# A two-layer fp32 trunk on one core: the decay's narrow projection taken from the normed tiles, within the third value group

## The chip, the core and the metric

One core of one Trainium2 chip. The metric is the device time of one execution in microseconds, as a median over runs. All values are fp32, and the result has to have fp32 accuracy, which decides how products are formed (below).

## The reference, cut to what matters

A trunk of two layers. Each layer has a feed-forward part, a mixer stage with four branches (convolution, retention, gated linear attention, differential attention over a paged cache), and another feed-forward part. It works on 592 tokens: 64 of samples, 16 meta tokens, 512 of a prompt. The mixer stage starts with one projection of the normed activations, of which the gated branch's decay takes 16 columns:

```python
x = rmsnorm(h, w['norm_mix'])
z = x @ w['w_in'] + w['b_in']
(c_a, c_g, r_q, r_k, r_v, r_g, g_q, g_k, g_v, g_r, g_low,
 d_q, d_k, d_v, gates) = jnp.split(z, split_at, axis=-1)
...
g_pre = (g_low @ w['gla_alpha_w'] + w['gla_alpha_b']).astype(jnp.float32)
gla_decay = (jax.nn.log_sigmoid(g_pre) / GLA_TAU).reshape(B, L, GLA_HEADS, GLA_DK)
```

`g_low` has 16 columns; it is the narrow projection that is meant here.

## The kernel before

**Layout.** Activations lie transposed: 128 partitions by 8 blocks (KD) of 592 tokens (T). A product of fp32 accuracy is made from parts: a tile x is split into `x_hi` (rounded) and `x_lo` (the rest), weights likewise into `w_hi` and `w_lo`, and TensorE makes hi x hi, hi x lo and lo x hi in a fast format. The narrow projection is the exception: its weights `low_raw` are whole fp32, and TensorE multiplies them in its whole-fp32 form. Its 592 tokens are cut into four strips of 148, and strip r takes the 32 columns of the array, and the 32 output rows, from 32 r on. PSUM has eight banks; a pair of them holds a product of 592 tokens.

**Queues.** Every engine runs a list written out by hand, with waits on semaphores between them. A wait stops everything behind it on its engine. Weights come in units of 128 x 1024 through a ring of four slots: SyncE loads, ScalarE makes `w_hi` (`split_high`, L814), VectorE makes `w_lo` (`split_low`, L2063).

**The stage around the change** is `project(l)`, which every engine has; it runs once for each layer, at 423 to 500 us and again some 1391 us later.

- TensorE: three value groups of 256 columns each, over five windows of tokens. Products of a group go to banks (5 g + w) mod 8 (L1626). Group 0 works with activations that aren't scaled by the norm. Group 1 as well. Group 2 runs block by block: for each block k, 15 matmuls (five windows by three parts), and then it signals `x_taken`, since nobody needs the unscaled block k any more. Then come tiles 0 to 3 of the transposed projections (`tile(l, c)`, L1420), each 48 matmuls into a bank pair, tile c into pair min(c, 3). Then the narrow projection (L1677) into bank 0: for each of 8 blocks, for x_hi and x_lo, four strips; 64 matmuls. Then tile 4 (`Z_FIRST`), which takes pair 3 like tile 3 and waits for ScalarE's eviction of tile 3. Then sums of squares for the attention's norms (L1432).
- VectorE: evicts the five windows of each group with scale and bias (L2425), then splits two weight units. Behind group 1's splits it runs `renorm(l)`: for each block it writes the normed tile, whole, into one of three rooms `fresh[k % 3]` (L2087), and once ScalarE has copied it rounded to `x_hi` (L855, behind `x_taken`), it makes `x_lo` for block k-1 (L2081). Then group 2's evictions.
- ScalarE: `renorm` copies; `split_high` of two units; eviction of tiles 0 to 3 (L1082), each followed by a `split_high`; then a wait for the narrow product, its eviction in four strips to `GL` (L1100), and then the squares of tiles 0 to 3 (L1117), which open the attention.
- GpSimd loads the value bias and `low_raw` at the start of the stage (L714, L715).

TensorE's narrow block and its neighbours:

```python
                pe.wait_ge(low_loaded, 16)
                pe.wait_ge(z_ready, 1)
                for k in range(KD):
                    for n, xp in enumerate((x_hi, x_lo)):
                        for r in range(4):
                            mm = pe.matmul(ps[32 * r:32 * r + 32, 0, 0:STRIP], low_raw[:, k, :], xp[:, k, STRIP * r:STRIP * r + STRIP].bitcast(F32),
                                           start=k == 0 and n == 0, stop=k == KD - 1 and n == 1)
                mm.then_inc(low_product, 1)
```

Of the kernel before, what the change touches and what calls it, by code (L numbers as in the profile page):

```python
# [19 lines left out]
F32 = mybir.dt.float32  # L20
# [4 lines left out]
ACT = mybir.ActivationFunctionType  # L25
# [5 lines left out]
KD, KF = D // P, FF // P  # L31
# [3 lines left out]
T = TS + META + SEQ  # L35
# [89 lines left out]
Z_FIRST, Z_BEFORE = 4, 6  # L125
# [73 lines left out]
def build(nc, h_in, wstream, wlow, params, vbias, cache_k, cache_v, page_table, st_ret, st_gla,  # L199
# [9 lines left out]
    with ExitStack() as ctx:  # L209
        def sem(name):  # L210
            return ctx.enter_context(nc.semaphore(name))
# [7 lines left out]
        def keep(name, shape, dt=F32):  # L219
            nonlocal at  # L220
            t = place(name, shape, dt, at)
            at += -(-4 * int(np.prod(shape[1:])) // 32) * 32
            return t

        hT = keep("hT", [P, KD, T])
        x_hi = keep("x_hi", [P, KD, T], F32R)
        x_lo = keep("x_lo", [P, KD, T], F32R)
# [94 lines left out]
        GL = V[96:112, 0, 0:T]  # L322
        inverse_room, fresh = Z[:, 10, :], (Z[:, 11, :], Z[:, 12, :], Z[:, 13, :])
# [8 lines left out]
        kpage = area("kpage", [P, 2, PAGES, 2 * P], 0)  # L332
        vpage = area("vpage", [P, 2, PAGES, 256], 16384)
        low_raw = area("low_raw", [P, 8, 32], 32768)
        STRIP = T // 4
        vb = area("vb", [P, 768], 45056)
        s_bias = area("s_bias", [P, PAST + NT], 32768)
        new_bias = area("new_bias", [P, 4, TS], 36896)
# [78 lines left out]
        ps = ctx.enter_context(nc.psum_tensor("ps", [P, 8, 512], F32))  # L417
# [19 lines left out]
        normed = sem("normed")  # L437
# [25 lines left out]
        def msem(name):  # L463
            cleared.append(sem(name))
            return cleared[-1]

        v_products, v_ready, z_ready = msem("v_products"), msem("v_ready"), msem("z_ready")
        low_loaded, low_product = msem("low_loaded"), msem("low_product")
# [338 lines left out]
        def _(act):  # L807
# [280 lines left out]
            def project(l):  # L1088
                act.wait_ge(mixers_open, l + 1)
                act.sem_inc(phases_entered, 1)  # L1090
                norm(l, 1)
                for c in range(-6, -2):
                    tile(l, c)
                renorm(l)
                for c in range(-2, Z_FIRST):
                    tile(l, c)
                act.wait_ge(low_product, 1)
                for r in range(4):
                    r0 = 32 * r
                    ins = act.activation(GL[:, STRIP * r:STRIP * r + STRIP], ps[r0:r0 + 16, 0, 0:STRIP], ACT.Identity,  # L1100
                                         bias=prm[r0:r0 + 16, P_ZB + NZ:P_ZB + NZ + 1])
                ins.then_inc(z_ready, 1)

            def exps(x):
                n = META if x < H else P
# [303 lines left out]
        def _(pe):  # L1409
# [170 lines left out]
            def tile(l, c):  # L1580

                pos = c + 6
                unit_ready(l * QUADS + U_MIX // RING + pos // RING, pos % RING)
                if c == Z_FIRST:
                    pe.wait_ge(z_ready, Z_FIRST)
                elif c == Z_FIRST + 1:
                    pe.wait_ge(z_ready, Z_FIRST + 1)
                    pe.wait_ge(root_logs, 3)
                elif c == Z_BEFORE:
                    pe.wait_ge(z_ready, Z_FIRST + 2)  # L1590
                elif c > Z_BEFORE:
                    pe.wait_ge(z_ready, c + 1)
                if c:
                    products(z_pair(c), pos % RING, (0, 8), 0, x_hi, x_lo).then_inc(units_multiplied, 1)
                else:
                    for k in range(KD):
                        pe.wait_ge(x_ready, l * 16 + 8 + k + 1)
                        last = products(0, pos % RING, (k, k + 1), k, x_hi, x_lo, start=k == 0, stop=k == KD - 1)
                    last.then_inc(units_multiplied, 1)
# [17 lines left out]
            def project(l):  # L1617
                pe.wait_ge(mixers_open, l + 1)
                pe.sem_inc(phases_entered, 1)

                def values(g, w, k):

                    c0, n = window(w)
                    s0 = 2 * g % RING
                    for m, (xp, wp) in enumerate(((x_hi, w_hi), (x_hi, w_lo), (x_lo, w_hi))):
                        mm = pe.matmul(ps[0:n, (WINDOWS * g + w) % 8, 0:256], xp[:, k, c0:c0 + n], wp[:, s0:s0 + 2, k, :],  # L1626
                                       start=k == 0 and m == 0, stop=k == KD - 1 and m == 2)
                    return mm

                def value_done(mm, w):  # L1630
                    mm.then_inc(*((v_products, 1) if w < WINDOWS - 1 else (units_multiplied, 2)))

                unit_ready(l * QUADS + U_MIX // RING, 1)
                pe.wait_ge(x_ready, l * 16 + KD - 1)
                for k in range(KD):
                    if k == 3:
                        pe.wait_ge(squares_summed, 8 * (l * 3 + 2))
                        sum_tile(3, ones[:, 0, :], ssum)
                        for w in range(WINDOWS):
                            c0, n = window(w)  # L1640
                            mm = pe.matmul(ps[0:n, 5, w:w + 1], ssum[:, c0:c0 + n], ones[:, 0, 0:1], start=True, stop=True)
                        mm.then_inc(square_total, 1)
                    if k == KD - 1:
                        pe.wait_ge(x_ready, l * 16 + KD)
                    for w in range(WINDOWS):
                        mm = values(0, w, k)
                        if k == KD - 1:
                            value_done(mm, w)
                pe.wait_ge(norm_steps, 2 * (l * 3 + 1) + 1)
                pe.wait_ge(token_steps, 2)  # L1650
                unit_ready(l * QUADS + U_MIX // RING, 3)
                for w in range(WINDOWS):
                    if WINDOWS + w >= 8:
                        pe.wait_ge(v_ready, WINDOWS + w - 7)
                    for k in range(KD):
                        mm = values(1, w, k)
                    value_done(mm, w)
                unit_ready(l * QUADS + U_MIX // RING + 1, 1)
                pe.wait_ge(v_ready, 3 * WINDOWS - 8)
                for k in range(KD):  # L1660
                    for w in range(WINDOWS):
                        mm = values(2, w, k)
                        if k == KD - 1:
                            value_done(mm, w)
                    if k < KD - 1:
                        mm.then_inc(x_taken, 1)
                pe.wait_ge(v_ready, 2 * WINDOWS)
                tile(l, 0)
                pe.wait_ge(v_ready, 3 * WINDOWS)
                for c in range(1, Z_FIRST):  # L1670
                    tile(l, c)
                pe.wait_ge(low_loaded, 16)
                pe.wait_ge(z_ready, 1)
                for k in range(KD):
                    for n, xp in enumerate((x_hi, x_lo)):
                        for r in range(4):
                            mm = pe.matmul(ps[32 * r:32 * r + 32, 0, 0:STRIP], low_raw[:, k, :], xp[:, k, STRIP * r:STRIP * r + STRIP].bitcast(F32),  # L1677
                                           start=k == 0 and n == 0, stop=k == KD - 1 and n == 1)
                mm.then_inc(low_product, 1)

            prompt_heads = [(j, h) for j in range(WINDOWS) for h in range(H)]

# [349 lines left out]
            for n, c in enumerate(range(0, RL, 512)):  # L2032
                mm = pe.matmul(ps[0:16, 4 + n, 0:min(512, RL - c)], rb[0:33, :], bucket[0:33, c:min(c + 512, RL)], start=True, stop=True)
            mm.then_inc(bias_row_made, 1)
            for n in range(SQUARED_FIRST):
                pe.wait_ge(squared, n + 1)
                mm = sum_tile(1, ident[:, :], square_rooms[:, n, :], start=n == 0, stop=n == SQUARED_FIRST - 1)
# [19 lines left out]
        def _(v):  # L2057
# [16 lines left out]
            def renorm(l):  # L2074

                v.wait_ge(norm_steps, 2 * (l * 3 + 1) + 2)

                def low(k):
                    v.wait_ge(x_high, 16 * l + 8 + k + 1)
                    v.wait_ge(normed, 8 * l + k + 1)  # L2080
                    v.tensor_tensor(x_lo[:, k, :], fresh[k % 3], x_hi[:, k, :].bitcast(F32), ALU.subtract).then_inc(x_ready, 1)  # L2081

                for k in range(KD):
                    c = P_GAIN + 8 + k
                    if k >= 3:
                        v.wait_ge(x_ready, 16 * l + 8 + k - 2)
                    v.scalar_tensor_tensor(fresh[k % 3], hT[:, k, :], prm[:, c:c + 1], inverse_room, ALU.mult, ALU.mult).then_inc(normed, 1)  # L2087
                    if k:
                        low(k - 1)
                low(KD - 1)  # L2090
# [341 lines left out]
            def tile(l, c):  # L2432

                pos = c + 6
                split_low(l * QUADS + U_MIX // RING + pos // RING + 1, pos % RING)
# [741 lines left out]
```

## Time and profile before

| | |
|---|---|
| median of 3 runs | 2790.12 us |
| lowest, highest | 2789.74, 2792.55 us |
| the profiled execution, first to last instruction | 2789.1 us |
| TensorE busy | 2767.2 us (99%) |
| VectorE busy | 1986.8 us (71%) |
| ScalarE busy | 1206.8 us (43%) |
| mean granted clock of TensorE | 0.998 |
| one layer's narrow block on the chain | 4.16 us |

The rows further down come from one profiled execution, in microseconds from its first instruction. PE is TensorE's matmul, PEld its weight load, DVE VectorE, ACT ScalarE, POOL GpSimd. L1677 is line 1677 of the kernel. In a timeline a row gives the start, the length, and how many instructions are merged into it; matmuls overlap in the array, so a matmul's length is more than its distance to the next. A matmul of whole fp32 leaves two records. An entry in brackets is the engine's idle time before the row and who ended it. The chain is the work that ended last, followed back from the end of the kernel.

### The profile page before, as it was taken

What the parts mean: (1) busy time and instruction counts of PE and PEld (TensorE: products, weight loads), DVE (VectorE), ACT (ScalarE), POOL (GpSimd) and SP (SyncE); (2) the same over time, 40 slices, a digit from 0 to 9 for tenths busy, and PEclk for the clock granted to TensorE, in tenths of its full rate; (3) what the DMA queues carried; (4) which work ended last, traced back from release to release, by engine and by line L of the source; (5) the groups of instructions that cost most, each with busy time, mean ns of one, the idle gap of its engine ahead of it and who ended that gap; (6) DMA issues with size and microseconds to landing.
All of it is one profiled execution on the core that took longest, in us unless ns stands there. A gap on an engine that the chain in (4) does not pass through costs nothing.

```text
span 2789.1 us, 57776 instructions
## 1 busy us (share of the span) xinstructions
PE 2767.2 (99%) x21828; PEld 2687.1 (96%) x21828; DVE 1986.8 (71%) x3589; ACT 1206.8 (43%) x2160; POOL 128.2 (5%) x234
## 2 busy tenths in 40 slices
PE   8999999999999999999999999999999999999999
PEld 7999999998899999999999999999888999999999
DVE  8889534478667688887488895344787676899952
ACT  6445323435435254445254453234354343544521
POOL 0000001230000000000000000012300000000000
PEclk9999999999999999999999999999999999999999
DMA  4222326463234312223212223255733343122233
GB/s 138 91 95 98 108 75 198 155 202 131 98 117 172 140 64 91 90 90 114 91 67 92 90 98 106 68 198 163 214 118 121 108 178 130 61 92 103 98 106 103
DMA packets 104815, 325.92 MB, mean 117 GB/s; under 512 B 15055, under 2 KB 31855, under 8 KB 103104
## 3 DMA queue, kind: packets, MB, share of 16 engines
q1 hardware_dynamic: 91728, 280.67, 29.2%
q0 software_dynamic: 12912, 42.86, 4.8%
q8 instruction: 118, 1.93, 0.3%
q14 instruction: 57, 0.47, 0.1%
HBM read 291.45 MB, written 30.94 MB: 116 GB/s over the span
## 4 chain that ended last, share of the span: by engine, by line
PE 98%; DVE 1%; ACT 1%; issue 0%; DMA 0%; DVEq 0%; ACTq 0%; POOLq 0%
PE ps L1420 52%; PE ps L1449 35%; PE ps L1626 3%; PE ps L1432 1%; PE ps L1695 1%; PE ps L1911 1%; PE ps L1747 1%; PE ps L1728 1%; PE ps L1775 0%; PE ps L1795 0%; PE ps L1677 0%; PE ps L1737 0%; PE ps L1851 0%; PE ps L1934 0%; PE ps L1777 0%
## 5 line engine op out<-in xcount | busy, mean ns | idle before, releaser
L2063 DVE TENSOR_TENSOR w_lo<-w_raw,w_hi 128x1024 fp32r<-128x1024 f32 x240 | 292.7, 1224 | 353.0 <-ACT w_hi L814 349.4
L1449 PE MATMUL ps<-x_more,w_hi 128*128 128x296 f32 (+1 forms) x2112 | 456.8, 298 | 1.2 <-DVE x_more L2927 0.8
L1449 PE MATMUL ps<-x_hi,w_hi 128*128 128x296 f32 (+1 forms) x1408 | 420.0, 298 | 1.2 <-DVE w_lo L2101 1.2
L1449 PE MATMUL ps<-x_hi,w_lo 128*128 128x296 f32 (+1 forms) x1408 | 420.4, 299 | 0.0
L1449 PE MATMUL ps<-x_lo,w_hi 128*128 128x296 f32 (+1 forms) x1408 | 420.4, 299 | 0.0
L814 ACT ACTIVATE w_hi<-w_raw 128x1024 fp32r<-128x1024 f32 x224 | 234.9, 1053 | 407.2 <-PE ps L1420 240.1
L1420 PE MATMUL ps<-x_hi,w_hi 128*128 128x296 f32 (+1 forms) x1600 | 362.4, 308 | 3.8 <-ACT hT L1162 3.8
L2101 DVE TENSOR_TENSOR w_lo<-w_raw,w_hi 128x512 fp32r<-128x512 f32 x440 | 296.6, 690 | 88.4 <-ACT w_hi L862 85.8
L1449 PEld LDWEIGHTS ps<-x_more,w_hi 128*128 128x128 f32 x2112 | 351.0, 188 | 2.4 <-issue 1.3
L1420 PE MATMUL ps<-x_hi,w_lo 128*128 128x296 f32 (+1 forms) x1600 | 347.3, 299 | 0.0
L1420 PE MATMUL ps<-x_lo,w_hi 128*128 128x296 f32 (+1 forms) x1600 | 347.2, 298 | 0.0
L1449 PE MATMUL ps<-x_more,w_lo 128*128 128x296 f32 (+1 forms) x1056 | 314.6, 298 | 0.0
L1420 PE MATMUL ps<-hid_hi,w_hi 128*128 128x296 f32 (+1 forms) x1408 | 309.4, 299 | 0.0
L1420 PE MATMUL ps<-hid_lo,w_hi 128*128 128x296 f32 (+1 forms) x1408 | 307.8, 297 | 0.0
L1420 PE MATMUL ps<-hid_hi,w_lo 128*128 128x296 f32 (+1 forms) x1408 | 307.8, 297 | 0.0
L912 ACT ACTIVATE p_copy<-ps 128x296 f32<-128x296 f32 (+1 forms) x264 | 109.7, 416 | 389.2 <-PE ps L1449 388.8
L1420 PEld LDWEIGHTS ps<-x_hi,w_hi 128*128 128x128 f32 x1600 | 257.7, 189 | 20.1 <-issue 15.8
L862 ACT ACTIVATE w_hi<-w_raw 128x512 fp32r<-128x512 f32 x440 | 265.4, 623 | 14.1 <-PE ps L1420 13.4
L1449 PEld LDWEIGHTS ps<-x_hi,w_hi 128*128 128x128 f32 x1408 | 265.8, 189 | 2.0 <-DVE w_lo L2101 1.7
L1449 PEld LDWEIGHTS ps<-x_hi,w_lo 128*128 128x128 f32 x1408 | 265.9, 189 | 0.1
L1449 PEld LDWEIGHTS ps<-x_lo,w_hi 128*128 128x128 f32 x1408 | 265.1, 188 | 0.0
L1420 PEld LDWEIGHTS ps<-x_hi,w_lo 128*128 128x128 f32 x1600 | 260.2, 189 | 0.0
(378 smaller groups left out, 4926.9 us busy)
## 6 DMA issues: line engine op xcount, KB each, us to landing
w_raw<-wstream SPq DMA_DIRECT2D x420, 512.0 KB, 3.6
kpage<-cache_k SPq DMA_DIRECT2D x128, 128.0 KB, 3.1
vpage<-cache_v POOLq DMA_DIRECT2D x128, 128.0 KB, 3.8
gate_rows<-hT SPq DMA_DIRECT2D x48, 296.0 KB, 2.3
d_sg<-gate_rows SPq DMA_DIRECT2D x16, 888.0 KB, 5.3
h_rows<-hT SPq DMA_DIRECT2D x2, 2368.0 KB, 9.5
hT<-h_rows SPq DMA_DIRECT2D x2, 2368.0 KB, 8.7
hT<-h_in SPq DMA_DIRECT2D x4, 592.0 KB, 8.3
```

The lines of the kernel that those rows point to most:

```text
L814: act.activation(w_hi[:, slot, :, :], w_raw[:, slot, :, :], ACT.Copy).then_inc(weights_high, 1)
L862: act.activation(w_half(t)[0], w_source(t, g, total), ACT.Copy).then_inc(operands_high, 1)
L912: act.activation(room[:, 0:span()], ps[:, bank, 0:span()], ACT.Copy).then_inc(pair_taken, 1)
L1420: mm = pe.matmul(ps[:, 2 * p + half, 0:cols], wp[:, k, :], xp[:, k0 + k - blocks[0], half * cols:(half + 1) * cols], start=start and k == ...
L1432: mm = pe.matmul(ps[:, 2 * p + half, 0:span()], mat, tile[:, half * span():(half + 1) * span()], start=start, stop=stop)
L1449: mm = pe.matmul(ps[:, bank, 0:span()], wp[:, k, :], xp, start=new and k == 0 and n == 0, stop=k == KH - 1 and n == 2, skip_group_check=True)
L1626: mm = pe.matmul(ps[0:n, (WINDOWS * g + w) % 8, 0:256], xp[:, k, c0:c0 + n], wp[:, s0:s0 + 2, k, :], start=k == 0 and m == 0, stop=k == KD ...
L1695: mm = pe.matmul(ps[0:n, score_bank(j, g, i), 0:min(ns, 512)], q, k[:, 0:min(ns, 512)], start=True, stop=True)
L1728: mm = pe.matmul(ps[r0:r0 + 32, part, :], q, kpage[:, b2, 4 * part:4 * part + 4, P * j:P * j + P], start=True, stop=True)
L1747: pe.matmul(ps[r0:r0 + 32, 5, 0:P], s_turn[:, s, r0:r0 + 32], vpage[:, b2, s, P * j:P * j + P], start=s == 0, stop=False)
L2063: v.tensor_tensor(w_lo[:, slot, :, :], w_raw[:, slot, :, :], w_hi[:, slot, :, :].bitcast(F32), ALU.subtract).then_inc(weights_low, 1)
L2101: v.tensor_tensor(lo, w_source(t, g, total), hi.bitcast(F32), ALU.subtract).then_inc(weight_steps, 1)
```

## The change

The block of 64 narrow matmuls behind tile 3 is gone. Instead, within the third value group, TensorE issues behind the 15 value matmuls of block k four narrow matmuls of block k, which read the normed tile whole from VectorE's room `fresh[k % 3]` and accumulate in bank 7; there are 32 in a layer. Before each portion TensorE waits for the room of its block (`normed`), before the first also for the loaded weights and for the eviction of bank 7. Each portion signals `low_product`, and VectorE waits for it before it writes over a room. ScalarE evicts the narrow product ahead of tile 0 instead of behind tile 3, so the counts that `z_ready` is waited for shift by one, and tile 3, which takes bank 7, waits for that eviction. Everything else stays as it was.

```diff
@@ -332,7 +332,7 @@
         kpage = area("kpage", [P, 2, PAGES, 2 * P], 0)
         vpage = area("vpage", [P, 2, PAGES, 256], 16384)
         low_raw = area("low_raw", [P, 8, 32], 32768)
-        STRIP = T // 4
+        STRIP, LOW_BANK = T // 4, 7
         vb = area("vb", [P, 768], 45056)
         s_bias = area("s_bias", [P, PAST + NT], 32768)
         new_bias = area("new_bias", [P, 4, TS], 36896)
@@ -1092,14 +1092,16 @@
                 for c in range(-6, -2):
                     tile(l, c)
                 renorm(l)
-                for c in range(-2, Z_FIRST):
+                for c in range(-2, 0):
                     tile(l, c)
-                act.wait_ge(low_product, 1)
+                act.wait_ge(low_product, KD)
                 for r in range(4):
                     r0 = 32 * r
-                    ins = act.activation(GL[:, STRIP * r:STRIP * r + STRIP], ps[r0:r0 + 16, 0, 0:STRIP], ACT.Identity,
+                    ins = act.activation(GL[:, STRIP * r:STRIP * r + STRIP], ps[r0:r0 + 16, LOW_BANK, 0:STRIP], ACT.Identity,
                                          bias=prm[r0:r0 + 16, P_ZB + NZ:P_ZB + NZ + 1])
                 ins.then_inc(z_ready, 1)
+                for c in range(Z_FIRST):
+                    tile(l, c)
 
             def exps(x):
                 n = META if x < H else P
@@ -1581,8 +1583,10 @@
 
                 pos = c + 6
                 unit_ready(l * QUADS + U_MIX // RING + pos // RING, pos % RING)
-                if c == Z_FIRST:
-                    pe.wait_ge(z_ready, Z_FIRST)
+                if c == Z_FIRST - 1:
+                    pe.wait_ge(z_ready, 1)
+                elif c == Z_FIRST:
+                    pe.wait_ge(z_ready, Z_FIRST + 1)
                 elif c == Z_FIRST + 1:
                     pe.wait_ge(z_ready, Z_FIRST + 1)
                     pe.wait_ge(root_logs, 3)
@@ -1664,19 +1668,19 @@
                             value_done(mm, w)
                     if k < KD - 1:
                         mm.then_inc(x_taken, 1)
+                    if k == 0:
+                        pe.wait_ge(low_loaded, 16)
+                        pe.wait_ge(v_ready, LOW_BANK + 1)
+                    pe.wait_ge(normed, 8 * l + k + 1)
+                    for r in range(4):
+                        mm = pe.matmul(ps[32 * r:32 * r + 32, LOW_BANK, 0:STRIP], low_raw[:, k, :], fresh[k % 3][:, STRIP * r:STRIP * r + STRIP],
+                                       start=k == 0, stop=k == KD - 1)
+                    mm.then_inc(low_product, 1)
                 pe.wait_ge(v_ready, 2 * WINDOWS)
                 tile(l, 0)
                 pe.wait_ge(v_ready, 3 * WINDOWS)
                 for c in range(1, Z_FIRST):
                     tile(l, c)
-                pe.wait_ge(low_loaded, 16)
-                pe.wait_ge(z_ready, 1)
-                for k in range(KD):
-                    for n, xp in enumerate((x_hi, x_lo)):
-                        for r in range(4):
-                            mm = pe.matmul(ps[32 * r:32 * r + 32, 0, 0:STRIP], low_raw[:, k, :], xp[:, k, STRIP * r:STRIP * r + STRIP].bitcast(F32),
-                                           start=k == 0 and n == 0, stop=k == KD - 1 and n == 1)
-                mm.then_inc(low_product, 1)
 
             prompt_heads = [(j, h) for j in range(WINDOWS) for h in range(H)]
 
@@ -2084,6 +2088,7 @@
                     c = P_GAIN + 8 + k
                     if k >= 3:
                         v.wait_ge(x_ready, 16 * l + 8 + k - 2)
+                        v.wait_ge(low_product, k - 2)
                     v.scalar_tensor_tensor(fresh[k % 3], hT[:, k, :], prm[:, c:c + 1], inverse_room, ALU.mult, ALU.mult).then_inc(normed, 1)
                     if k:
                         low(k - 1)
```

## Rows read from the trace of the kernel before

**Rows 1.** The page's first lines and the chain by engine: busy time (share), share of the chain.

```profile
span 2789.1 us, 57776 instructions
...
PE 2767.2 (99%) x21828; PEld 2687.1 (96%) x21828; DVE 1986.8 (71%) x3589; ACT 1206.8 (43%) x2160; POOL 128.2 (5%) x234
...
PE 98%; DVE 1%; ACT 1%; issue 0%; DMA 0%; DVEq 0%; ACTq 0%; POOLq 0%
```

**Rows 2.** Waits of TensorE, 425 to 700 us: total, times, longest.

```profile
PE ps L1420 <- ACT hT L1162: 1.9, 3, 0.9
```

**Rows 3.** The chain in order of time, 425 to 600 us: start, us, what.

```profile
467.97 26.25 PE ps L1420 x192
494.21 4.16 PE ps L1677 x128
498.38 6.76 PE ps L1420 x48
```

**Rows 4.** Timeline of TensorE around the narrow block: start, us, line, operation, count.

```profile
493.78 0.43 PE L1420 MATMUL ps<-x_lo,w_hi 128*128 128x296 f32 x2
494.14 0.46 PE L1677 MATMUL ps<-x_hi,low_raw 128*32 128x148 f32 x8
...
497.94 0.43 PE L1677 MATMUL ps<-x_lo,low_raw 128*32 128x148 f32 x8
498.31 0.54 PE L1420 MATMUL ps<-x_hi,w_hi 128*128 128x296 f32 x2
498.69 0.43 PE L1420 MATMUL ps<-x_hi,w_lo 128*128 128x296 f32 x2
```

**Rows 5.** Timeline of TensorE, third value group: first matmuls of blocks 0 and 1.

```profile
453.73 0.28 PE L1626 MATMUL ps<-w_hi,x_hi 128*80 128x256 f32 x1
...
455.46 0.28 PE L1626 MATMUL ps<-w_hi,x_hi 128*80 128x256 f32 x1
```

**Rows 6.** Timeline of VectorE as the third value group begins.

```profile
455.09 2.36 DVE L2063 TENSOR_TENSOR w_lo<-w_raw,w_hi 128x1024 fp32r<-128x1024 f32 x2 [0.67 <-ACT w_hi L814]
457.37 1.58 DVE L2087 SCALAR_TENSOR_TENSOR Z<-hT,prm,Z 128x592 f32<-128x592 f32 x2
459.02 0.78 DVE L2081 TENSOR_TENSOR x_lo<-Z,x_hi 128x592 fp32r<-128x592 f32 x1
459.71 0.83 DVE L2087 SCALAR_TENSOR_TENSOR Z<-hT,prm,Z 128x592 f32<-128x592 f32 x1
```

**Rows 7.** Timeline of ScalarE: copies of the rooms, eviction of tile 3.

```profile
458.29 1.45 ACT L855 ACTIVATE x_hi<-Z 128x592 fp32r<-128x592 f32 x2 [2.29 <-DVE Z L2087]
...
494.25 0.76 ACT L1082 ACTIVATE Z<-ps,prm 128x592 f32<-128x592 f32 x1 [4.86 <-PE ps L1420]
```

**Rows 8.** Timelines of VectorE and ScalarE at the same two places, second layer.

```profile
1848.33 1.58 DVE L2087 SCALAR_TENSOR_TENSOR Z<-hT,prm,Z 128x592 f32<-128x592 f32 x2
...
1885.21 0.76 ACT L1082 ACTIVATE Z<-ps,prm 128x592 f32<-128x592 f32 x1 [4.86 <-PE ps L1420]
```

**Rows 9.** Timeline of TensorE: value products behind the one-column products.

```profile
430.75 0.33 PE L1626 MATMUL ps<-w_hi,x_hi 128*80 128x256 f32 x1
430.91 0.28 PE L1626 MATMUL ps<-w_lo,x_hi 128*80 128x256 f32 x1
```

**Rows 10.** Stretches: length, busy PE PEld DVE ACT POOL, granted clock, DMA share, GB/s.

```profile
737.00:740.00 3.00, 3.00 (x13) 2.78 (x13) 1.98 (x5) 0.14 (x1) 0.00 (x0) 0.50 0.02 5
740.00:744.00 4.00, 4.00 (x26) 3.15 (x25) 0.81 (x2) 0.00 (x0) 0.00 (x0) 0.54 0.64 197
2126.00:2129.50 3.50, 3.50 (x17) 3.22 (x18) 2.10 (x5) 0.00 (x0) 0.00 (x0) 0.51 0.08 13
```

**Rows 11.** The chain, 722 to 748 us.

```profile
737.83 3.26 PE ps L1420 x12
```

**Rows 12.** GpSimd's issue of the narrow weights, and its us to landing.

```profile
429.50 0.54 POOL L715 DMA_DIRECT2D low_raw<-wlow  x1
...
low_raw<-wlow POOLq DMA_DIRECT2D x1, 128.0 KB, 10.7
```

## The prediction, made before the changed kernel ran

> **What bounds the kernel now.** I read the page first. TensorE is busy 99% of a span of 2789.1 us and holds 98% of the chain that ended last [rows 1]. In such a kernel a microsecond counts only if TensorE loses or gains it. The waits of TensorE say whether later slack could swallow a loss. From 425 to 700 us, which is the first layer's projection and attention, their longest account is 1.9 us for ScalarE's L1162, in three pieces, and what else it waited for is shorter than a microsecond [rows 2]. Nothing behind the projection waits for a DMA, so a delay of TensorE there moves the end by the same amount.
>
> Then I read the chain through the projection, in order of time [rows 3]. Tiles 0 to 3 take 26.25 us, 6.56 each, the narrow projection 4.16 us (128 records; every whole fp32 matmul leaves two, so 64 matmuls), and tile 4 behind it 6.76 us, 0.20 more than a tile that follows a tile. The second layer does the same 1390.96 us later, to 0.01 us [rows 6 to 8]. So I work out one layer and double it. The profiled span is 1.0 us under the median of 2790.12, so differences carry over as they are.
>
> **Removed: the block behind tile 3.** 64 matmuls go, with both of their transitions: 4.16 + 0.20 = 4.36 us a layer.
>
> **Added: 32 matmuls in eight portions.** The old block shows the price of a portion. Sixteen rows of four matmuls (eight records) start between 494.14 and 497.94, 15 steps of 0.253 us [rows 4]. Eight portions cost 8 x 0.253 = 2.03 us. Using the normed tile whole therefore saves 2.0 us of streaming; moving it has to be paid from that.
>
> **Added: eight ways into the 32-column form and out of it, where there was one.** The old block shows one such passage. The last pair of tile 3 starts at 493.78; pairs are 0.274 apart (6.56 / 24), so the next would start at 494.05, but the first narrow matmul starts at 494.14: 0.09. On the way out, the last portion starts at 497.94 and would be through at 498.19; tile 4 starts at 498.31: 0.12. Its first pair takes 0.38 to the next instead of 0.27: 0.11 [rows 4]. The first portion is also 0.03 longer. Together 0.35 us. The floor is the other change of form in this stage, from one-column products back to the value products: their first start-to-start is 0.16 instead of 0.12, some 0.05 [rows 9], though these keep 80 or more columns of the array. Between 0.05 and 0.35 I take 0.30, near the narrow block's own passage, a little less because a value product streams 256 columns against weights of 80 behind each portion. Eight passages: 2.4 us (0.4 to 2.8).
>
> The Trainium skill, TensorEngine Tiling, section Tiling Modes, has a rule against this change: going from one tiling mode to another drains the array. A full drain at both ends is a rival below. Page and rows agree that each passage costs something; the page names no price.
>
> **Added: the wait for the first normed tile.** In the third value group TensorE now waits, behind block 0 of the values, for the first of VectorE's rooms. Block 0 starts at 453.73 and block 1 at 455.46 [rows 5], so the first portion would start at about 455.55. VectorE's order is unchanged: it first splits two weight units from 455.09 (2.36 us), and the first room is started at 457.37 and, at 0.83 for a room, done by 458.20; ScalarE, which waits for that same room, starts on it at 458.29 [rows 6, 7]. TensorE can be released no earlier: 458.29 - 455.55 = 2.75 us a layer. Queued behind that wait are all other blocks of values and tile 0. I see no work that covers it; before, TensorE ran through block 0 and block 1 without needing the rooms at all.
>
> From block 1 on nobody should wait. A TensorE block becomes 1.73 + 0.25 + 0.30 = 2.3 us. VectorE needs for a step one room (0.75 from start to start) and one low part (0.78), and between them lies ScalarE's copy of 0.70, so from the freeing of x_hi[k-2] to room k it is 0.09 + 0.70 + 0.78 + 0.83 = 2.4 us, while TensorE takes 4.6 for the same two blocks [rows 6, 7]. VectorE's added wait (room k mod 3 is not overwritten before portion k-3) asks for a portion three blocks old; behind it are queued the low parts, the evictions of the values and two weight splits, which tile 1 and tile 2 need, but it has long been granted when VectorE comes to it. Cost nothing; if it did bite, each block would lose the difference to 2.3. The weights low_raw are issued at 429.50 and take 10.7 us [rows 12], so they are there 15 us ahead of their new use. GpSimd's queue is not moved.
>
> **Moved: the eviction of tile 3 loses its cover.** Tiles 3 and 4 use the same pair of banks, so tile 4 waits for ScalarE's eviction of tile 3. That ran from 494.25 to 495.01, while TensorE was in the narrow block. Without the block TensorE would want tile 4 at 494.06 and gets it at about 495.10, with 0.09 for the signal as seen at 458.29 [rows 4, 7]: 1.04 us a layer, new. ScalarE's four small reads of the product move ahead of tile 0's eviction, six microseconds in which it was idle, and VectorE's and TensorE's next steps (squares, sums) keep at least the distance they had. Bank 7 is read out long before tile 3 wants it. Both at nothing.
>
> **Sum.** Per layer -4.36 + 2.03 + 2.40 + 2.75 + 1.04 = +3.86 us; both layers +7.7 us, so 2790.12 + 7.7 = 2797.8. With passages at 0.05 it is +1.86 a layer, 2793.8; with 0.35, and 0.1 more for tile 4 starting after a wait, +4.36 a layer, 2798.8.
>
> **Rivals.**
> 1. Passages are cheap among value products (0.05). For it: rows 9, and the value form has shorter matmuls. Against: the narrow block's own passage of 0.35. Gives 2793.8, inside what counts as no change.
> 2. Full drain at each switch. A value product starts 0.12 after the one before (1.73 / 15) but lasts 0.28 [rows 5], so a way in would cost 0.16; a narrow one lasts about 0.29 behind the start of its portion's last matmul, so a way out costs 0.26. 8 x 0.42 = 3.4 instead of 2.4, +1.0 a layer: 2799.8. Against it, the passage in rows 4 took 0.09 in and 0.12 out. This is the skill's rule in full strength; the trace bears out a fraction of it.
> 3. The clock falls at the new gap. It does fall elsewhere: to 0.50 of full, which is 1.2 instead of 2.4 GHz, at 737 and 2126 us [rows 10], behind runs of small matmuls in retention. Twelve big matmuls then took 3.26 us [rows 11] instead of 1.64 (six pairs at 0.274). A gap of 2.75 us is idle where those runs were at least busy, which speaks for it; no gap of this length stands inside the warm part of this trace, so its level after one is not shown. If 3.4 us run at the lower level, that costs about 1.6 us, in one layer or in both: 2799.4 to 2801.0.
> 4. The other side, not slower: the falls of the clock in retention go away. They are there in both layers of this execution, and they may hang on when the small runs come. The stretches put the first at 3 us and 92% of 4 more, 6.7 us, the second at 3.4 us [rows 10]; work bound by the array loses half of that, 5.0 us, the small matmuls less, so I take 4.5 in all. If the shifted program misses both, +7.7 - 4.5 = +3.2: 2793.3, no change by measure. With cheap passages as well, +3.7 - 4.5 = -0.8: 2789.3. It decides only if the falls are missed in most of the runs; the three runs of before span 2.8 us, so single runs do differ by such amounts.
> 5. The change does what it says and nobody waits, because room 0 comes ahead of its need. Then only streaming counts: 2 x (2.03 - 4.36) = -4.7 us plus passages, 2785.4 to 2790.2. It would need room 0 by 455.55, and VectorE's order puts it at 458.20.
>
> **How the numbers follow.** A difference under 0.2% (5.6 us) is about what a measurement of this kernel can't tell from none. Chances: forecast 2797.8 at 0.52; rival 1 at 0.15; rival 2 at 0.08; rival 3 at 0.16; rival 4 at 0.06; rival 5 at 0.03. Slower by over 0.2% (above 2795.7) holds the forecast and rivals 2 and 3: 0.76. Same: rivals 1 and 4 and most of 5: 0.21. Faster: 0.03. Range 2793.5 to 2801.0: from passages at their floor to clock falls in both layers.
>
> **What would show it.** In the changed kernel's waits of TensorE a new row must stand: the narrow matmul waits for VectorE's room, some 2.7 us, twice. A second: L1420 waits for ScalarE's L1082, about 1 us, twice. On the chain the value products and the portions from the start of block 0 to tile 0 must take 14.2 + 2.75 + 4.4 = 21.4 us instead of 14.2, and tile 4 must follow tile 3 without a block between. If the steps from block to block are near 2.0 us, rival 1 is right; near 2.5, rival 2; if the granted clock shows 0.5 behind the gap, rival 3. I am wrong if the first wait is absent or is paid back later by a wait of before that shrinks, which rows 2 leave little room for.

## The result

The changed kernel takes 2801.91 us (median of 5 runs, 2799.03 to 2803.39) against 2790.12 (5 runs, the three of the table above and two more, 2787.82 to 2792.55). The ratio is 1.004, with a 95% interval from 1.0029 to 1.0051: slower by 8 to 14 us. The forecast was 2797.8 with a range from 2793.5 to 2801.0. The direction is right, the time lies 0.9 us above the range, and the median is 4.1 us above the forecast.

The profiled execution spans 2801.7 us, 12.6 more than the one of before. First the page, its busy times and the chain by engine:

```profile
span 2801.7 us, 57532 instructions
...
PE 2771.6 (99%) x21700; PEld 2685.0 (96%) x21700; DVE 1986.7 (71%) x3589; ACT 1206.9 (43%) x2160; POOL 128.6 (5%) x234
...
PE 97%; DVE 1%; ACT 1%; issue 0%; DMA 0%; SPq 0%; DVEq 0%; ACTq 0%
```

TensorE holds 97% of the chain, nearly as much as in [rows 1]. Its matmul count fell by 128 records: 32 matmuls in each of two layers, two records each. Then its waits over the whole span (total, times, longest), where before only the second of these three rows stood (its part in the first mixer stage is in [rows 2]):

```profile
PE ps L1676 <- DVE Z L2092: 5.4, 2, 2.7
PE ps L1422 <- ACT hT L1164: 3.8, 6, 0.9
PE ps L1422 <- ACT Z L1082: 1.9, 2, 0.9
```

Both waits that the prediction named are there, twice each: 2.7 us for VectorE's first room and 0.9 us for the eviction of tile 3. Neither took anything from the old wait for L1164 (L1162 of before): 1.9 us in each mixer stage, as before.

The chain through the first layer's projection (start, us, what), to be laid beside [rows 3]. Everything up to here runs 0.06 us later than before, as VectorE's splits show (455.15 here, 455.09 in [rows 6]):

```profile
454.06 1.07 ACT w_hi L814
...
455.15 2.36 DVE w_lo L2067 x2
457.51 0.76 DVE Z L2092
...
458.40 0.70 PE ps L1676 x8
459.11 3.21 PE ps L1630 x15
462.31 0.39 PE ps L1676 x8
462.70 1.92 PE ps L1630 x15
464.62 0.39 PE ps L1676 x8
465.01 1.94 PE ps L1630 x15
...
476.19 0.39 PE ps L1676 x8
476.58 26.45 PE ps L1422 x192
...
503.05 0.76 ACT Z L1082
...
503.95 6.80 PE ps L1422 x48
```

The chain now leaves TensorE: it goes through ScalarE's and VectorE's weight splits and the first room (0.76 us), and only then back to the first portion. From 462.31 on a block and its portion take 2.27 to 2.33 us (464.62 - 462.31 = 2.31). Before, a block alone took 1.78 on average: the eight of them filled the 14.24 us from 453.73 [rows 5] to 467.97 [rows 3]. But the first block behind the gap takes 3.21 us, where the next takes 1.92. Tile 4 starts at 503.95; before it started at 498.38, so the first layer loses 5.5 us (5.57 less the 0.06). The forecast had 3.9.

What made that one block slow is in the stretches (length, busy PE PEld DVE ACT POOL, granted clock, DMA share, GB/s):

```profile
454.00:458.00 4.00, 1.68 (x15) 1.49 (x13) 3.33 (x4) 2.01 (x2) 3.53 (x8) 1.00 0.78 212
458.00:461.80 3.80, 3.40 (x21) 2.98 (x22) 2.52 (x4) 0.70 (x1) 2.45 (x5) 0.56 0.97 334
1849.00:1854.80 5.80, 3.27 (x29) 3.08 (x27) 3.54 (x5) 2.01 (x2) 5.13 (x10) 0.98 0.72 198
1854.80:1858.40 3.60, 3.40 (x23) 2.99 (x23) 2.31 (x4) 0.70 (x1) 2.69 (x5) 0.56 0.98 360
816.00:824.00 8.00, 8.00 (x58) 6.71 (x55) 2.01 (x5) 1.77 (x3) 0.00 (x0) 0.57 0.40 142
2207.00:2217.00 10.00, 10.00 (x79) 8.45 (x77) 3.75 (x6) 2.14 (x4) 0.00 (x0) 0.66 0.48 151
```

Up to the first gap the granted clock is 1.00. In the 3.8 us behind it the mean is 0.56, most of them at 1.2 instead of 2.4 GHz, and nearly the same at the second layer's gap. The trace puts the two falls at 458.48 to 461.89 us and at 1854.53 to 1857.94, so the first begins just behind the start of the first portion (458.40) and the second 0.46 us ahead of it (1854.99), while TensorE still waits. The last two rows are other falls of the clock, in later stages, at half for 6.8 us of each stretch (8 x 0.43 x 2 is 6.9, 10 x 0.34 x 2 is 6.8); before had such falls too, of 6.8 and 3.4 us (the first and the third row of [rows 10] begin in them). The second layer's chain, and the start of its tile 4 in the kernel before:

```profile
1854.99 0.72 PE ps L1676 x8
1855.71 2.95 PE ps L1630 x15
...
1859.05 1.92 PE ps L1630 x15
...
1900.30 4.75 PE ps L1422 x33
```

```profile
1889.34 6.76 PE ps L1420 x48
```

The first block there takes 2.95 us. Tile 4 comes 1900.30 - 1889.34 = 10.96 us later than before; VectorE's splits of that stage, which start ahead of the gap, come 1851.74 - 1846.05 = 5.69 us later. So the second layer's projection loses 5.3 us. The row of before:

```profile
1846.05 2.36 DVE L2063 TENSOR_TENSOR w_lo<-w_raw,w_hi 128x1024 fp32r<-128x1024 f32 x2 [0.67 <-ACT w_hi L814]
```

The span grew by 12.6. If the two profiles are laid side by side, VectorE's instructions in order, what comes on top of the two layers is the other falls. The changed kernel is 5.7 us late at 700 us and 2.7 us from 745 on, because before pays there for its fall of 6.8 us. It is 5.7 us late again behind its own fall at 817. In the second layer the lateness goes from 11.1 us to 9.6 (the fall of 3.4 us in before) and to 12.6 (the fall of 6.8 us at 2210 here), and stays there to the end. A fall of 6.8 us so cost 3.0 us there and one of 3.4 us 1.5, and the changed kernel had 13.7 us of such falls where before had 10.2. They vary from one execution to the next in both kernels.

### The profile page after: what moved, and what is told of

Its sections match the earlier page's. It is cut to its first block, busy times and chain, and to the rows that moved or that the text cites. A ratio compares the mean times of both kernels' runs of the same rounds, so it can differ in the third digit from the quotient of the medians.

```text
span 2801.7 us, 57532 instructions
## 1 busy us (share of the span) xinstructions
PE 2771.6 (99%) x21700; PEld 2685.0 (96%) x21700; DVE 1986.7 (71%) x3589; ACT 1206.9 (43%) x2160; POOL 128.6 (5%) x234
## 3 DMA queue, kind: packets, MB, share of 16 engines
q8 instruction: 117, 1.92, 0.3%
## 4 chain that ended last, share of the span: by engine, by line
PE 97%; DVE 1%; ACT 1%; issue 0%; DMA 0%; SPq 0%; DVEq 0%; ACTq 0%
PE ps L1422 51%; PE ps L1451 35%; PE ps L1630 3%; PE ps L1434 1%; PE ps L1699 1%; PE ps L1915 1%; PE ps L1751 1%; PE ps L1732 1%; PE ps L1779 0%; PE ps L1799 0%; DMA w_raw<-wstream 0%; PE ps L1741 0%; PE ps L1676 0%; PE ps L1938 0%; PE ps L1855 0%
```

## The experiments

Each comparison is against runs of the kernel before on the same chip, given as a difference of medians, with the interval of the ratio. Single executions of one kernel spread by 4 to 8 us, so a difference of medians under 1.5 us says little by itself; the profiles say more.

### The gap taken away: the first room ahead of the splits

```diff
                     if g == 1:
+                        v.wait_ge(norm_steps, 2 * (l * 3 + 1) + 2)
+                        room(l, 0)
                     for s in range(2):
                         split_low(quad + 1, 2 * g % RING + s)
```

(`room(l, 0)` is the same instruction that `renorm` issued first; `renorm` now begins with room 1.)

> The changed kernel, but VectorE writes the first normed room ahead of the two weight splits instead of behind them. Theory (the wait of 2.7 us per layer is real, and the low clock of some 3.4 us behind it is its consequence, 1.3 to 1.6 us per layer): both go, 2801.9 - 2 x (2.7 + 1.4) = 2793.7 us, no wait of the first portion, granted clock 1.00 at 455 to 465 us. Rival (the clock falls because of the many changes of form, not because of the gap): the wait goes, the low clock stays, 2796.5 us. Rival (the splits, now 0.8 us later, become the next wait): a new wait of tile 0 or 1 for w_lo, time above 2796.

Measured: 2794.32 us (11 runs) against 2790.91, +3.4 us, ratio 1.001 (1.0001 to 1.0019). TensorE's waits and the stretches behind the old gap, with the same columns as above:

```profile
PE ps L1422 <- ACT Z L1082: 1.9, 2, 0.9
...
PE ps L1676 <- DVE Z L2081: 0.6, 2, 0.3
```

```profile
455.00:462.00 7.00, 6.69 (x68) 5.54 (x68) 6.66 (x9) 2.92 (x4) 5.69 (x11) 1.00 0.89 278
462.00:475.00 13.00, 13.00 (x126) 11.18 (x125) 8.29 (x14) 5.60 (x8) 0.00 (x0) 1.00 0.42 141
```

The wait of 2.7 us is gone; 0.3 us a layer is left at portion 1, because the second room now stands behind the splits. No other wait appeared in the projection, so the later splits held nobody up. The clock holds at 1.00 through all eight passages of the first layer, and of the second as well (the trace has no fall there). So it was not the changes of form that lowered it. One VectorE instruction of 0.83 us, moved ahead of two of 1.22, is worth about 8 us (+11.8 against +3.4, each against before on its own chip), more than half of what the change lost. In the profiles the projection is 1.6 us a layer slower than before, against 5.5 and 5.3.

### The gap shortened: portions one block later

```diff
+                    if k:
+                        portion(k - 1)
+                portion(KD - 1)
-                    if k == 0:
-                        pe.wait_ge(low_loaded, 16)
...
-                    mm.then_inc(low_product, 1)
```

> The changed kernel, but portion k stands behind value block k+1 instead of behind block k, so TensorE has one block more to do before it needs the first room. Theory: the gap shrinks from 2.7 to about 1.0 us per layer, and behind so short a gap the clock holds: 2801.9 - 2 x (1.7 + 1.4) = 2795.7 us. Rival (any gap there lowers the clock, or the changes of form do): 2798.5 us with a granted clock of 0.5 for some 3.4 us.

Measured: 2794.84 us (11 runs) against 2790.91, +3.9, ratio 1.0015 (1.0006 to 1.0024). The wait, total, times and longest:

```profile
PE ps L1669 <- DVE Z L2098: 1.9, 2, 0.9
```

A gap of 0.9 us stays in each layer and the block behind it takes 1.92 us: the clock held. Shortening the gap by 1.8 us a layer gave 7.9 us in all (+11.8 against +3.9), or 6.9 by the two layers in the profiles (5.5 + 5.3 against 1.95 twice). That is about twice what the waiting alone could give (3.6).

### The gap filled, not shortened

```diff
                         pe.wait_ge(v_ready, LOW_BANK + 1)
+                        for n in range(22):
+                            pe.matmul(ps[:, LOW_BANK, 0:256], x_hi[:, KD - 1, 0:P], w_hi[:, 0:2, 0, :], start=True, stop=True)
                     pe.wait_ge(normed, 8 * l + k + 1)
```

> The changed kernel with 22 value-shaped matmuls of no use (128 x 256, into bank 7, which the first portion then starts afresh) ahead of the wait for the first room: they fill the 2.7 us that TensorE waited, and take away nothing of the waiting time. Theory (the gap lowers the clock): the first portion comes when it came, the clock stays at 1.00 behind it, 2801.9 - 2 x 1.4 = 2799.1 us. Rival (the clock does not hang on the gap): the low clock stays, 2801.9 us.

Measured: 2799.09 us (7 runs) against 2790.91, +8.2, ratio 1.0028 (1.0016 to 1.0039). The chain behind the gap:

```profile
458.10 0.46 PE ps L1678 x8
458.56 1.94 PE ps L1630 x15
```

The first portion comes about when it came in the changed kernel (0.1 us earlier, each counted from VectorE's splits), but takes 0.46 instead of 0.70 us, and the block behind it 1.94 instead of 3.21. With work of no use the kernel's median is 2.8 us lower: TensorE loses the waiting time either way, but not the clock. Since this compares across chips, the changed kernel, the filled one and a half filled one (11 matmuls, so that 1.4 us of waiting remain) were run together:

> The changed kernel as it is, beside the two kernels with a filled gap on the same chip, since the earlier comparison of the filled gap with it went across chips, and single executions differ by 2 to 4 us. Theory (the low clock behind the gap costs 1.4 us per layer): 11 to 12 us above before, and 2.8 above the filled gap. Rival (2.8 us was the chance of the executions): within 1 us of the filled gap.

> The filled gap as before (22 matmuls of no use). Theory: 8 to 9 us above before, 2.8 under the changed kernel beside it; clock 1.00 at 455 to 475 us. Rival: equal to the changed kernel.

> Half of the filler: 11 matmuls, so a gap of about 1.4 us stays ahead of the first portion. If the clock asks for the whole gap, as the gap of 0.9 us behind which it held suggests, it holds here as well, and the time is that of the fully filled kernel. If it falls at half the gap already, the time is that of the changed kernel, 2.8 us more, with a granted clock of 0.5 for 3.4 us.

Measured against 2790.67 (11 runs): changed 2801.91 (+11.2; 5 runs; 1.0023 to 1.0051), filled 2798.95 (+8.3; 6 runs; 1.0018 to 1.0043), half filled 2798.62 (+8.0; 6 runs; 1.0016 to 1.0041). The intervals overlap; the medians differ by 3.0 and 3.3 us in the direction expected. Of all ten runs of the changed kernel seven took more than 2801.5 us, of all thirteen with the filled gap one, of the six with the half filled gap two. The firmer evidence is in the profiles. The half filled kernel, behind its two remaining gaps of 1.4 us:

```profile
455.00:462.00 7.00, 5.62 (x57) 4.82 (x56) 5.67 (x7) 2.70 (x4) 5.89 (x12) 1.00 0.82 278
...
1854.00:1862.00 8.00, 6.97 (x71) 5.87 (x72) 6.27 (x9) 2.09 (x3) 3.51 (x7) 1.00 0.96 319
```

1.00 in both layers. The changed kernel, profiled a second time, was more instructive: in its first layer the clock held, in its second it fell, from 1853.50 on (0.73 us ahead of the first portion) for 6.8 us.

```profile
455.00:462.00 7.00, 4.28 (x45) 3.51 (x44) 5.68 (x7) 2.58 (x4) 5.64 (x11) 1.00 0.87 270
...
1854.00:1862.00 8.00, 7.77 (x55) 6.31 (x56) 3.87 (x6) 1.80 (x3) 2.54 (x5) 0.60 0.96 319
```

So a gap of 2.7 us doesn't lower the clock every time. In the profiles of the changed kernel (two) and of the one with other banks (one, below) there are six such gaps; behind five the clock fell, for 3.4 us in four cases and for 6.8 in the one just shown. It didn't always fall at once. In the kernel with other banks the first portions start at 458.02 and 1850.37, and the lower clock begins 1.3 and 1.6 us later. These are its stretches, in the columns used above:

```profile
459.28:462.69 3.41, 3.41 (x22) 2.74 (x21) 1.65 (x4) 0.70 (x1) 1.62 (x3) 0.50 0.99 356
1851.92:1855.33 3.41, 3.41 (x23) 2.73 (x22) 1.89 (x3) 0.70 (x1) 1.08 (x2) 0.50 0.96 290
```

Two blocks share the loss there (2.74 and 2.31 us in the first layer, 2.50 and 2.54 in the second). Behind the gaps of 1.4 us (two) and 0.9 us (two), and behind the filled ones (four), it never did. The first layer of the changed kernel's second profile shows the change without the clock's part:

```profile
458.53 0.46 PE ps L1676 x8
458.99 1.94 PE ps L1630 x15
...
475.20 26.45 PE ps L1422 x192
...
502.57 6.79 PE ps L1422 x48
```

Its origin is 0.19 us later than that of before (VectorE's splits start at 455.28). Portion 0 starts at 458.53 - 0.19 = 458.34, 2.79 us after the 455.55 at which TensorE would have wanted it; tile 4 starts at 502.38 against 498.38: 4.0 us for the layer, where 3.86 were forecast. The second layer of the same profile lost 6.6 us, so the fall of 6.8 us cost 2.6.

### Tile 4 in another pair of banks

```diff
-        QK_BANKS = (1, 2, 0, 1)
+        QK_BANKS = (1, 3, 0, 1)
...
-            return 0 if c == Z_FIRST + 1 else min(c, 3)
+            return {Z_FIRST: 2, Z_FIRST + 1: 0}.get(c, min(c, 3))
...
-                    pe.wait_ge(z_ready, Z_FIRST + 1)
+                    pe.wait_ge(z_ready, Z_FIRST)
```

(and the small lambda product in bank 2 instead of 4)

> The changed kernel with other banks: tile 4 in pair 2 instead of pair 3, the second sum of squares in pair 3 instead of pair 2, and the small lambda product in bank 2. Tile 4 then needs only tile 2's eviction. Theory (the lost cover of tile 3's eviction costs 0.95 us per layer): the wait of L1422 for L1082 goes, 2801.9 - 1.9 = 2800.0 us. Rival (tile 4's wait is paid back by ScalarE's lead behind it): 2801.9 us and a new wait at the sums of squares or at tile 5.

Measured: 2800.21 us (6 runs) against 2790.91, +9.3, ratio 1.0033 (1.0021 to 1.0046). The wait for L1082 is gone from TensorE's waits and no other took its place; the chain runs from tile 0 through tile 4 without a break, 240 matmuls in 32.99 us. The median is 1.7 us under that of the changed kernel (2.5 by the differences to before), as expected, but that difference is within the spread of single executions; shown is the wait's disappearance, not its price to the tenth. In the profile the clock fell behind both gaps, and the projection lost 4.3 us in each layer, against 5.5 and 5.3.

### Both waits taken away

The two edits together (the first room ahead, and tile 4 in pair 2).

> The changed kernel with both new waits taken away: the first room ahead of the weight splits, and tile 4 in pair 2. What is left of the change is 32 matmuls fewer and seven passages more per layer. Theory: per layer -4.36 + 2.03 + 8 x 0.3 = +0.1 us, so 2790.2 us, no different from before; the eight passages alone eat what the halved streaming saves. Rival (passages cost little): 2786 to 2788 us.

Measured: 2792.02 us (11 runs) against 2792.29, ratio 1.000 (0.9991 to 1.0009). What is left of the change is 32 matmuls fewer and eight portions with their passages, and by the runs that sums to nothing that can be told from before. In the profile the projection is 0.4 us a layer slower: the forecast's terms give +0.1, and the wait of 0.3 us at portion 1 is still there.

### One portion of 32, from eight rooms

```diff
-        inverse_room, fresh = Z[:, 10, :], (Z[:, 11, :], Z[:, 12, :], Z[:, 13, :])
+        inverse_room, fresh = Z[:, 10, :], tuple(Z[:, n, :] for n in (11, 12, 13, 5, 6, 7, 8, 9))
```

with `fresh[k]` for `fresh[k % 3]`, VectorE's wait for `low_product` gone, and the 32 matmuls behind the third value group, ahead of tile 0.

> The changed kernel with eight rooms instead of three, so that all 32 narrow matmuls run in one block behind the third value group, ahead of tile 0: one passage into the 32-column form and out of it instead of eight, and no wait for the first room. Tile 4's wait for tile 3's eviction stays. Theory (a passage costs 0.3 us, the gap 2.7, the low clock 1.4): per layer against before -4.36 + 2.03 + 0.35 + 0.95 = -1.0 us, so 2790.1 - 2.1 = 2788.0 us; against the first-room-early kernel (8 passages, 2793.7) the difference is 7 passages in each layer, 2 x 7 x 0.3 = 4.2 us, plus small change. Rival (passages are cheap, and the rest of the loss lies in the room traffic of VectorE and ScalarE beside them): less than 1.5 us under the first-room-early kernel.

Measured: 2789.01 us (11 runs) against 2792.29, -3.3, ratio 0.9988 (0.9979 to 0.9997). The chain:

```profile
468.04 2.15 PE ps L1676 x64
470.19 26.45 PE ps L1422 x192
```

The 32 matmuls take 2.15 us, and the tiles behind them 26.45 instead of 26.25: one passage costs 2.15 + 0.20 - 2.03 = 0.32 us. Against the kernel with the early first room the median is 5.3 us lower, but the two ran on different chips; the differences to before are 6.7 us apart. Seven passages a layer at 0.30 and the 0.3 us of waiting that was left there make 2 x 2.4 = 4.8. The profiles give 4.9: the projection is 0.87 us a layer faster than before here, and 1.6 slower there. The rival, that the loss is in the room traffic, is out: the copies and low parts are the same here.

### The old place, from eight rooms

The kernel before, with the same eight rooms, and:

```diff
+                pe.wait_ge(normed, 8 * l + KD)
                 for k in range(KD):
-                    for n, xp in enumerate((x_hi, x_lo)):
-                        for r in range(4):
-                            mm = pe.matmul(ps[32 * r:32 * r + 32, 0, 0:STRIP], low_raw[:, k, :], xp[:, k, STRIP * r:STRIP * r + STRIP].bitcast(F32),
+                    for r in range(4):
+                        mm = pe.matmul(ps[32 * r:32 * r + 32, 0, 0:STRIP], low_raw[:, k, :], fresh[k][:, STRIP * r:STRIP * r + STRIP],
```

> The kernel before, with the narrow block at its old place behind tile 3, but from eight whole rooms: 32 matmuls instead of 64. No portion, no gap, and tile 3's eviction stays covered (the block takes 2.0 us, the eviction 1.0). Theory: 2790.1 - 2 x 2.03 = 2786.0 us, faster than both kernels. Rival (something else, such as ScalarE's reading of the narrow product ahead of the squares, takes the place of the streaming): between 2788 and 2790.1 us with a wait of the sums of squares for ScalarE.

Measured: 2788.25 us (11 runs) against 2792.29, -4.0, ratio 0.9986 (0.9977 to 0.9995): faster than before, and 0.5% faster than the changed kernel by the ratios to before. The 2788.25 would fit the rival's 2788 to 2790.1 as well, but before took 2792.29 on this chip, the difference is the theory's (-4.1), and no wait of the sums of squares is in the profile. The chain:

```profile
468.09 26.25 PE ps L1420 x192
494.34 2.15 PE ps L1677 x64
496.49 6.76 PE ps L1420 x48
```

The block is 2.15 us instead of 4.16 [rows 3], 2.0 us less in each layer, and tile 4 follows without a wait: a block of 2.15 us is still longer than the eviction it covers. This has the whole gain of the change, the halved streaming, and neither its passages nor its two waits. Its profile still spans 2789.2 us, 0.1 more than that of before. The projections gained 2.0 us each, but this execution had 17.1 us of clock falls in the later stages where that of before had 10.2, which cost it 3.0 us more, and TensorE waited 0.3 and 0.5 us for a DMA of `kpage` in the attention:

```profile
PE ps L1728 <- DMA kpage<-cache_k: 0.8, 2, 0.5
```

Slower kernels had such waits too (0.8 us with the half filled gap), so they aren't shown to come from this edit. It needs five more rooms, which lie in tiles of Z that are written only behind tile 4's eviction.

## Why the prediction was right and where it was wrong

**Removed and added streaming: right.** 4.16 us of block went. The portions with their passages cost 4.45 us a layer in the profile without a low clock: there tile 0 starts at 475.20 - 0.19 = 475.01, 7.04 us later than in [rows 3]; 2.79 of that is the gap, which leaves 4.25, and the tiles behind take 26.45 instead of 26.25, 0.20 more. Forecast: 2.03 + 2.40 = 4.43. That it fits to 0.02 us is partly luck: 0.30 was a choice between 0.05 and 0.35, and the reason given for it, the value products' 256 columns, wasn't put to a run. Rivals 1 (0.05 a passage) and 2 (0.42, a full drain to the recorded end) are both out. One passage among value products, from the timeline of TensorE:

```profile
464.34 0.28 PE L1630 MATMUL ps<-w_hi,x_lo 128*128 128x256 f32 x1
464.55 0.46 PE L1676 MATMUL ps<-Z,low_raw 128*32 128x148 f32 x8
464.94 0.34 PE L1630 MATMUL ps<-w_hi,x_hi 128*80 128x256 f32 x1
465.12 0.28 PE L1630 MATMUL ps<-w_lo,x_hi 128*80 128x256 f32 x1
```

In: the next value product would start at 464.34 + 0.12 = 464.46, the portion starts at 464.55, 0.09 later. Out: 464.94 - 464.55 = 0.39 against 0.25 for a portion, 0.14; the next start 0.18 later instead of 0.12, 0.06. That is 0.29 here. The Trainium skill's statement in TensorEngine Tiling, section Tiling Modes, that a change of mode drains the array, agrees with the trace in that every passage costs. A wait until the last matmul's recorded end would have been 0.16 and 0.26, and it was 0.09 and 0.14; these ends are modelled, so that the array drains is not refuted by this.

**The wait for the first room: right**, 2.72 us as the profile counts it, forecast 2.75. **From block 1 on nobody waits: right**, the steps are all 2.3 us. The 1.73 us that the prediction has for a block is the first one's; they average 1.78, so a step of 2.32 leaves 0.29 for the passage.

**Tile 4's wait: right in place, slightly short in size.** 0.92 us on the chain instead of 1.04, but tile 4 takes 6.79 us behind a wait too, so the 0.20 that I had booked as saved with the old block's way out did not come back. Together 0.1 us a layer more than the sum, which the bound had allowed for. ScalarE's reads of the narrow product moved ahead of tile 0's eviction at no cost. Its idle time there was not the six microseconds that the prediction named, but 4.0 us before, behind the weight splits; 1.54 us of reads fit into it:

```profile
478.85 1.54 ACT L1100 ACTIVATE V<-ps,prm 16x148 f32<-16x148 f32 x4
...
503.05 0.75 ACT L1082 ACTIVATE Z<-ps,prm 128x592 f32<-128x592 f32 x1 [4.86 <-PE ps L1422]
```

**No payback later: right.** No wait of before shrank.

**The step that failed is the clock behind the new gap, which the sum carries at nothing.** The sum books the gap of 2.75 us and lets TensorE go on at full clock behind it. The fall was in the text as rival 3 with its price, 1.6 us in one layer or both, and it measured 1.5 and 1.3 in the profiled execution (5.5 and 5.3 us for the layers against 4.0), and 0 and 2.6 in the second one. What was mis-sized is its chance: 0.16, and it showed behind five of six gaps. The rows had pointed to the fall, and the prediction says so itself: at 737 us the clock fell although TensorE was not idle at all but busy with small matmuls, so "not shown" should not have been read as unlikely. With rival 3 as the forecast the sum is 2790.1 + 8.0 + 2.8 = 2800.9, a microsecond from the median. The rest of the profile's 12.6 us is 1.5 for the other falls and some 0.3 in small pieces outside the projections.

**The range was cut too short above.** Its upper end was the central sum plus the clock in both layers. The bounds of the other terms were not added to it, nor the falls of the clock that come and go elsewhere, which move single executions by several microseconds (the medians of before, on the chips used here, run from 2790.12 to 2792.29). Rival 4, that these falls go away, did not come true: both profiles of the changed kernel have 13.7 us of them, that of before 10.2. But they do come and go: the profile of the kernel with other banks has 3.4 us of them, at 2796.13 us. Its price for the falls of before, 4.5 us in all, was right (3.0 and 1.5). The 0.2% that the prediction took for the limit of a measurement was too coarse: the interval of the result is 0.11% to either side. And the 0.21 given for "same" is the sum of rivals 1 and 4 alone, without rival 5.

## What to carry to other kernels

Work that is cut into portions and put between an engine's other work pays for a change of the array's form at every portion, and it inherits the timing of whoever feeds it. Count the passages, and look up when the first operand is made, before counting what is saved. Here halving the streaming was worth 4.0 us and could be had where the block already stood, by giving the operand more rooms; spread over eight places it was worth nothing, and with two uncovered waits and the clock's falls behind one of them it cost 11 to 12 us. Where a new gap opens on TensorE, book the clock with the gap, and look first at whether one instruction of the feeding engine can be moved ahead.

## What the runs showed of the hardware

- TensorE's clock fell to half behind a gap of 2.7 us in five of six cases, for 3.4 us, once for 6.8; the value block behind the gap took 2.50 to 3.42 us instead of 1.93, and in three cases the next one was slow as well. The fall began between 0.7 us ahead of the first matmul behind the gap and 1.6 us behind its start. Behind gaps of 1.4 and 0.9 us it held (two of each), and so it did where matmuls of no use filled the gap (four); the median with these was some 3 us lower.
- A change from the full array to 32-column strips and back cost 0.29 to 0.35 us in the places where it was measured, less than a drain to the recorded (modelled) end of the last matmul.
- Single executions differ with the granted clock's mean. In the second set of five runs of the changed kernel the two with 0.996 took 2803.82 and 2804.39 us, the one with 0.999 2797.53. Part of the spread that looks like noise in these kernels is the number of times the clock fell. What decides in which execution it falls in the later stages, behind small matmuls of retention and of the gated branch, and why it held behind one gap of six, is open; no run was made for it.
